# A two-block transformer step on one core: the ring of split weights begins 64 bytes behind a multiple of 128

## The reference, cut to what matters

```
z, xbc, dt_raw, q, kc, ... = split(rmsnorm(h, attn_norm_w) @ w_in)
h = h + mixed @ w_out
h = h + (silu(v @ w_gate) * (v @ w_up)) @ w_down          # FF width 5632
...
proj = rms_norm(x, norm_mix_pre) @ w_in_2
merged = sigmoid(g_a) * (y_hgrn @ w_up_a) + sigmoid(g_b) * (y_fox @ w_up_b)
x = x + rms_norm(merged @ w_o, norm_mix_post)
x = x + rms_norm((silu(gate) * up) @ w_ffn_down, norm_ffn_post)
```

## Time and profile before

| | us |
|---|---|
| median of 3 runs | 2567.81 (2567.69 to 2568.1) |
| profiled execution, its own time | 2569.16 |
| span of that execution, first to last instruction | 2565.9 |
| PE busy | 2553.9 (100%) |
| PEld busy | 2145.0 (84%) |
| DVE busy | 1510.8 (59%) |
| ACT busy | 1244.5 (49%) |
| DMA queue that carries the weights | 64.9% of 16 engines |

### The profile page before, as it was taken

The page is one execution under the profiler, slowest core; times in us unless marked ns, Lnnn a source line. Parts: engine busy times, 40 slices in busy tenths (PEclk is TensorE's granted clock), DMA queues, the critical chain, the costliest instruction groups (busy, mean ns, idle before and its releaser), DMA issues.

```text
span 2565.9 us, 32832 instructions
## 1 busy us (share of the span) xinstructions
PE 2553.9 (100%) x13330; PEld 2145.0 (84%) x13330; DVE 1510.8 (59%) x1807; ACT 1244.5 (49%) x1573; POOL 51.6 (2%) x68
## 2 busy tenths in 40 slices
PE   9999999999999999999999999999999999999998
PEld 9978888888888888898888888888888888888887
DVE  6777776555455555576568554556655545554555
ACT  5576645444344434465455454534544444443443
POOL 0151000000000000000000000000000000000000
PEclk9999999999999999999999999999999999999999
DMA  8554557777677667676655556576577766776664
GB/s 304 180 151 123 166 168 248 224 211 211 192 217 218 210 194 215 206 230 219 188 171 170 162 157 199 187 255 206 190 221 218 217 195 208 219 218 192 210 207 148
DMA packets 172839, 515.02 MB, mean 201 GB/s; under 512 B 17104, under 2 KB 48080, under 8 KB 171632
## 3 DMA queue, kind: packets, MB, share of 16 engines
q1 hardware_dynamic: 172544, 512.77, 64.9%
q10 hardware_dynamic: 144, 0.15, 0.0%
HBM read 492.54 MB, written 19.92 MB: 200 GB/s over the span
## 4 chain that ended last, share of the span: by engine, by line
PE 98%; DVE 1%; ACT 1%; issue 0%; DVEq 0%; ACTq 0%
PE ps L507 97%; PE ps L511 1%; DVE wlo L1691 0%; ACT W L1136 0%; ACT whi L1136 0%; DVE W L1691 0%; DVE W L2358 0%; ACT L1136 0%; DVE h L1694 0%; ACT scr L1136 0%; DVE W L2187 0%; DVE scr L1691 0%; DVEq L2675 0%; DVE RB L1764 0%; ACT sm L1136 0%
## 5 line engine op out<-in xcount | busy, mean ns | idle before, releaser
L1691 DVE TENSOR_TENSOR wlo<-raw,whi 128x1024 fp32r<-128x1024 f32 x884 | 1080.3, 1225 | 961.4 <-ACT whi L1136 956.9
L1136 ACT ACTIVATE whi<-raw 128x1024 fp32r<-128x1024 f32 x884 | 933.7, 1058 | 1092.6 <-PE ps L507 1081.0
L507 PE MATMUL ps<-whi,xx 128*128 128x512 f32 x4160 | 1285.5, 390 | 0.0
L507 PEld LDWEIGHTS ps<-whi,xx 128*128 128x128 f32 x4160 | 778.0, 188 | 160.6 <-issue 0.5
L507 PE MATMUL ps<-wlo,xx 128*128 128x512 f32 x2080 | 809.5, 389 | 0.0
L507 PEld LDWEIGHTS ps<-wlo,xx 128*128 128x128 f32 x2080 | 390.4, 188 | 81.6
L507 PE MATMUL ps<-whi,hlo 128*128 128x512 f32 x944 | 368.6, 390 | 0.0
L507 PE MATMUL ps<-wlo,hhi 128*128 128x512 f32 x944 | 367.4, 389 | 0.0
L507 PE MATMUL ps<-whi,hhi 128*128 128x512 f32 x944 | 367.3, 389 | 0.0
L507 PE MATMUL ps<-xx,whi 128*128 128x256 f32 (+1 forms) x1344 | 323.2, 334 | 0.1
L507 PE MATMUL ps<-xx,wlo 128*128 128x256 f32 x960 | 221.2, 280 | 0.1
(11 more groups left out here) (163 smaller groups left out, 915.5 us busy)
## 6 DMA issues: line engine op xcount, KB each, us to landing
raw<-in_gu SPq DMA_DIRECT2D x352, 512.0 KB, 4.3
raw<-in_w_in SPq DMA_DIRECT2D x256, 512.0 KB, 4.2
raw<-in_dn SPq DMA_DIRECT2D x176, 512.0 KB, 4.3
raw<-in_w_out SPq DMA_DIRECT2D x32, 512.0 KB, 3.7
raw<-in_w_up SPq DMA_DIRECT2D x32, 512.0 KB, 4.3
raw<-in_w_o SPq DMA_DIRECT2D x32, 512.0 KB, 4.3
W<-blocks SPq DMA_DIRECT2D x120, 128.0 KB, 2.7
blocks<-W SPq DMA_DIRECT2D x20, 512.0 KB, 6.4
```

Of the source, the lines that this page charges most:

```text
L507: return e.matmul(o, l, r, start=start, stop=stop, skip_group_check=skip)
L1136: return e.activation(o, i, f, **kw)
L1691: return e.tensor_tensor(o, a, b, op)
```

## The change

Two unused tensors of 16 floats (64 bytes per partition) are laid in front of and behind the ring:

```
         raw = sb("raw", [P, NRAW, 1024])
+        sb("gap0", [P, 16])
         whi = sb("whi", [P, NSPL, 1024], R)
         wlo = sb("wlo", [P, NSPL, 1024], R)
+        sb("gap1", [P, 16])
         xx = sb("xx", [P, KT, 2, T], R)
```

## The result

| | before | after |
|---|---|---|
| median of the runs, us | 2567.93 (4 runs) | 2623.28 (4 runs, 2622.11 to 2623.51) |
| ratio | | 1.0215, 95% interval 1.0199 to 1.023 |
| profiled execution, span, us | 2565.9 | 2621.6 |

The kernel became 55 us slower. That lies inside the stated range, but the forecast was no change, and it was wrong.

What follows compares the result with a forecast made beforehand. The prediction took the distance between TensorE product starts to bound the kernel. Every term was nothing, summing to 0 us: profiled execution 2569.16 us, median 2567.8 us; range 2558 to 2645 us, the forecast's own 2563 to 2573.

Steps and rivals of the forecast that it cites:

- What bounds the kernel: TensorE: time is the number of products times the distance between starts, 226.7 ns at 512 columns, including 13.3 ns fixed.
- The ring as moving operand: 9072 products streaming ring slots in rows of 512: no change from the offset; range 0 to +121 and 0 to -121 us.
- the addresses behind the ring: Everything behind the ring, 128 bytes higher, keeps its distance to multiples of 128: no change.
- The ring as stationary operand: 2304 products with a ring block in the array: no change; 15 us more if the price were 6.7 ns.
- rival B: TensorE products whose operands begin in different halves of 128 bytes become faster: -60 us, or -75 with stationary case; chance 0.08.
- The split: 884 ScalarE copies and 884 VectorE subtractions on the ring: no change, and covered by PE's time per unit.
- Rival A: Ring streams starting in mid-stretch touch 17 pieces of 128 bytes, not 16: +60 us or +121 us; chance 0.30.
- The weighing: Chances for the whole kernel's time: faster 0.12, same 0.52, slower 0.36.

Runs made afterwards that it cites:

- e13: Kernel before, first block's feed-forward part with 64 tokens in the array in place of 128 for all but a weight's first and last tile; 2577.22 us, ratio 1.0036.
- e14: Changed kernel, first block's feed-forward part with 64 tokens in the array in place of 128 for all but a weight's first and last tile; 2621.67 us, ratio 1.0209.
- e1: Against the kernel before, a gap in front of the ring only: ring and everything behind it begin 64 bytes behind a multiple of 128; 2568.35 us, ratio 1.0001.
- e11: Kernel before, with each 512-column product of the first block's feed-forward part made as two of 256; 2610.59 us, ratio 1.0165.
- e12: Changed kernel, with each 512-column product of the first block's feed-forward part made as two of 256; 2602.47 us, ratio 1.0133.
- e3: Against the kernel before, ring and everything behind it lie 128 bytes higher, all at multiples of 128; 2568.16 us, ratio 1.0.
- e15: Ring where the changed kernel has it, but 64 bytes further modulo 256 than what lies behind it, in place of 192; 2582.95 us, ratio 1.0059.
- e2: Against the kernel before, a gap behind the ring only: ring stays, everything behind it begins 64 bytes behind a multiple of 128; 2623.28 us, ratio 1.0215.
- e9: Layout with the ring 128 bytes further modulo 256 than everything behind it, all at multiples of 128; 2617.98 us, ratio 1.0193 to the kernel before.
- e4: Layout with `whi` 64 bytes behind a multiple of 128, `wlo` and everything behind it at a multiple; 2634.91 us, ratio 1.026 to the kernel before.
- e10: Against the kernel before, low halves of `xx` lie together, 64 bytes off the ring's grid; `hhi` and `hlo` unintentionally pushed by 128 bytes; 2609.65 us, ratio 1.0161.
- e18: As e17, but slots that stream begin 240 bytes further modulo 256 than the weight loads; 2638.82 us, ratio 1.0273 to the kernel before.
- e7: Layout with the ring 16 bytes behind a multiple of 128, the rest at multiples, `wlo` unintentionally 128 bytes further; 2604.32 us, ratio 1.0142 to the kernel before.
- e17: Against the kernel before, slots of 4352 bytes: streamed slots 0 bytes from the activations modulo 256, "feat" 64 and "half" 192 further; 2563.93 us, ratio 0.9982.

## Why the prediction was wrong, by its own steps

- **What bounds the kernel**: right. All of the change is in the distance between products; 6.5 ns over 9012 steps is 58 us, less 3 us in the other kinds, and no other engine had a part in it.
- **The ring as moving operand: "I take nothing"**: this step failed, together with the addresses behind the ring (below). It measured +58.3 us against 0. It rested on the earlier trace rows, where an offset of 64 bytes costs nothing. These rows are sound, but they change the offset of plain float32 streams at less than half the speed, and beside weight loads of 64 columns. Narrow loads shrink the price even at full speed (e13, e14). The prediction named the speed as a weakness and still took the value of the nearest row. What the runs showed in its place: a stream that begins 64 bytes less than the weight load takes 233.3 ns a step for 226.7, while a stream with the same offset beside a load with the same offset takes 226.7 (e1). The lower of the two prices that it kept for the range, +60 us from half of the fixed part, was nearly the result, and it is why the range holds the result. That is luck: it was worked out for a mechanism that e1 refutes.
- **The ring as stationary operand: nothing**: right that it costs nothing; it gained a little, 2.0 and 1.0 us., on which this rests, are rows of 256 columns beside loads of 60 and 120. They were used against rival B as well, and e11 and e12 show that rows of 256 answer to the place the other way round than rows of 512: they bounded nothing for the 9072 products.
- **The split, and the addresses behind the ring**: the split was right (1225 ns, 1059 ns). "`xx`, `hhi` and the rest keep their distance to multiples of 128, so by the rows above nothing changes" was wrong as an argument, since it is their distance to the ring that counts. It was wrong in effect too. With everything moved alike (e1, e3) nothing happens, but here the ring moved by 64 bytes and the rest by 128. In e15 the ring lies where the change put it and the rest is 256 bytes higher than before, the same place modulo 256: 15 us. With the rest 128 bytes higher it is 55 us. So some 40 of the 55 us (2623.28 less 2582.95) belong to this term, which the prediction put at nothing.
- **Rival A** gave the time nearly (2628 us for 2623) and the sign to look for (233 ns in "tok" alone), for a reason that e1, e2 and e12 refute. Had no layout but the changed one been run, A would have looked confirmed.
- **Rival B** named the right relation, the two operands of TensorE against each other, with the wrong sign. The two coincided before, and setting them apart by 64 bytes cost 55 us one way (192) and 15 us the other (e15), where B had a gain of 60 us.
- **The weighing** (a judgement, in hindsight): the profile showed a fixed part just as long as 128 bytes of stream, PE without slack and no comparable row. That should have put more on a dear outcome than 0.30.

The Trainium skill, "TensorE: Matmul & The Clock Gate", in its step-by-step section, says that the streamed operand and the weight load have read ports of their own, and that loading doesn't take bandwidth from the running product. No run here measures the bandwidth of a port, but the two reads are not independent in time: moving `xx`, `hhi` and all else behind the ring by 64 bytes while the ring stays (e2) costs 55 us, and moving them together with it (e1) costs nothing.

What stays open is the mechanism. Shown are: the place of the streamed operand relative to the weight load counts, and not the stream's own (e1, e2); 128 bytes apart is not the same as 0 (e9); the sign counts (e15); rows of 256 columns prefer the layout that rows of 512 pay for (e11, e12); neighbours count (e4, e10). The same place can also go with different steps for tens of microseconds on end (113.3 and 117.8 ns in e15, 233.3 and 236.7 ns in e18). No rule that gives all of these was found.

## What to carry to other kernels

Where TensorE streams float32r without a gap, look at the addresses of the streamed and the stationary operand together, modulo 256 bytes and not 128, and begin by keeping them equal for rows of 512 columns; an unused tensor of 64 bytes in the wrong place is worth 2% here. Measure it with both moved alike as a control, and for each width of row apart, since rows of 256 wanted the opposite. Other types at full speed were not tried. When the only rows with a property run at half the speed of the work in question, they bound nothing for it: go by the resource that is at its limit.

## What the runs showed of the hardware that was not expected

- A step of 512 float32r columns takes 226.7 ns with equal places and 233.3 in the changed layout; one of 256 takes 120.0 or 113.3. Each pair lies 6.7 ns apart, but steps between them occur too (228.9 in e15, 232.4 in e9), and a shorter one, the 225 ns from `whi` to `whi` in e7.
- Steps can be shorter with wider loads: 226.7 ns with 128 columns in the array, 229.6 on average with 64 (e13).
- The price is a matter of 16 bytes: e18 (D = 240) is 75 us slower than e17 (D = 0), which differs from it only by where units that aren't "feat" or "half" begin.
- A step's length can settle for tens of microseconds and change within one execution, as the 113.3 and 117.8 ns of "feat" in e15 do.
